# Mixture-of-experts loop of a hybrid decoder step: six whole-expert buffers, four tiles per turn in a skewed order, and no transfers for empty rows and empty blocks

## The reference

```
scores = sigmoid(t @ w_router); 64 experts in 8 groups, best 4 groups, best 8 experts per token
gates  = scores of the 8 chosen / their sum * 2.5
routed = sum over experts e: gates[:, e] * ((silu(t @ wg[e]) * (t @ wu[e])) @ wd[e])     # wg, wu 1024x256, wd 256x1024
shared = (silu(t @ w_sh_gate) * (t @ w_sh_up)) @ w_sh_down
x      = layernorm(alpha * x + g2 * (routed + shared))
```

## Time and profile before

| | |
|---|---|
| runs | 1959.46, 1959.55, 1952.16 us |
| profiled execution | 1952.46 us, span from first to last instruction 1950.6 us |
| the expert loop | from about 1137 us (first gate_up) to 1848.7 us |
| granted PE clock, mean over the span | 0.944 of full speed |

### The profile page before, as it was taken

How to read it: one execution, slowest core, us unless ns; L and a number is a source line. 1 busy time by engine, 2 the same in 40 slices (tenths; PEclk the granted TensorE clock), 3 DMA queues, 4 the chain that set the end, 5 groups by cost and what they waited for, 6 DMA issues and landing times.

```text
span 1950.6 us, 24171 instructions
## 1 busy us (share of the span) xinstructions
PE 1675.7 (86%) x8176; PEld 1041.8 (53%) x8176; DVE 639.6 (33%) x1421; ACT 408.3 (21%) x855; POOL 310.6 (16%) x571
## 2 busy tenths in 40 slices
PE   5999779988999899999969878888888888888713
PEld 2854558577857767888858633333333333333303
DVE  1213860587058842000145421111111111111186
ACT  1204431353135443000021111111111111111102
POOL 0002420255013400000001411111111111111100
PEclk8999889999999999999987989999999999999956
DMA  9113431211120083411011469999999999999681
GB/s 405 46 51 123 176 138 44 87 46 36 56 87 3 20 330 131 170 47 43 11 43 43 173 257 401 413 395 403 416 412 405 398 414 394 421 399 417 264 349 44
DMA packets 51051, 414.84 MB, mean 213 GB/s; under 512 B 5764, under 2 KB 9476, under 8 KB 23572
## 3 DMA queue, kind: packets, MB, share of 16 engines
q1 hardware_dynamic: 34276, 358.31, 46.3%
q0 software_dynamic: 14976, 54.50, 7.1%
q10 hardware_dynamic: 1728, 1.05, 0.2%
HBM read 372.91 MB, written 40.93 MB: 212 GB/s over the span
## 4 chain that ended last, share of the span: by engine, by line
PE 69%; DVE 13%; ACT 7%; issue 5%; DMA 3%; POOL 2%; ACTq 0%; SPq 0%; DVEq 0%; POOLq 0%
PE ps L1065 18%; PE ps L922 11%; PE ps L1086 10%; PE ps L883 9%; PE ps L868 7%; PE ps L954 3%; DVE work L1453 2%; DVE OA L1839 2%; ACT work L605 2%; ACT work L603 2%; DVE work L1442 1%; PE ps L839 1%; DMA W<-wq 1%; DVE work L1819 1%; PE ps L1077 1%
## 5 line engine op out<-in xcount | busy, mean ns | idle before, releaser
L1065 PE MATMUL ps<-W,work 128*64 128x512 f32 (+1 forms) x1200 | 357.0, 598 | 1.5 <-ACT work L1244 1.5
L1086 PE MATMUL ps<-work 128*64 128x512 f32 (+1 forms) x600 | 196.7, 639 | 64.1 <-ACT work L1259 64.1
L1065 PEld LDWEIGHTS ps<-W,work 128*64 128x64 f32 (+1 forms) x1200 | 129.9, 155 | 225.0 <-issue 225.0
L883 PE MATMUL ps<-Hb,W 128*128 128x260 f32 x768 | 172.9, 389 | 0.0
L883 PEld LDWEIGHTS ps<-Hb,W 128*128 128x128 f32 x768 | 148.5, 194 | 24.0 <-ACT work L1147 0.6
L1827 DVE COPY work<-ps 128x512 f32<-128x512 f32 x100 | 69.1, 691 | 269.0 <-PE ps L1086 269.0
L1086 PEld LDWEIGHTS ps<-work 128*64 128x64 f32 (+1 forms) x600 | 71.8, 163 | 157.9 <-issue 157.9
L1276 POOL TENSOR_TENSOR work<-work 128x128 f32<-128x128 f32 x168 | 82.8, 525 | 380.7 <-ACT work L605 380.3
L1250 ACT ACTIVATE work<-ps 128x256 f32<-128x256 f32 x50 | 19.2, 383 | 591.8 <-PE ps L1065 591.8
L1819 DVE TENSOR_TENSOR work<-ps,work 128x256 f32<-128x256 f32 x50 | 21.2, 424 | 358.6 <-ACT work L1250 358.6
L868 PE MATMUL ps<-W,Hb 128*128 128x512 f32 (+1 forms) x320 | 138.4, 592 | 0.0
(11 more groups left out here) (285 smaller groups left out, 2032.2 us busy)
## 6 DMA issues: line engine op xcount, KB each, us to landing
W<-wexp SPq DMA_DIRECT2D x76, 2048.0 KB, 11.8
work<-wexp SPq DMA_DIRECT2D x76, 1024.0 KB, 10.7
W<-wq SPq DMA_DIRECT2D x36, 2048.0 KB, 8.0
W<-yrows SPq DMA_DIRECT2D x6, 2048.0 KB, 16.9
work<-st_in SPq DMA_DIRECT2D x8, 1024.0 KB, 9.3
st_out<-work SPq DMA_DIRECT2D x8, 1024.0 KB, 7.1
Xb<-xT SPq DMA_DIRECT2D x2, 2080.0 KB, 17.9
work<-yrows SPq DMA_DIRECT2D x2, 2048.0 KB
```

The source lines that it names most:

```text
L883: mm = pe.matmul(ps[:, bank, 0:HALF], ring[:, q % 4, a, c, :], H[:, c, halves[b][0]:halves[b][1]], start=(c == 0), stop=(c == KC - 1))
L1065: mm = pe.matmul(ps[at, k, :], xe[:, k, c, at], GU[:, slot, c, :], start=(c == 0), stop=(c == KC - 1))
L1086: mm = pe.matmul(ps[at, 4 + hf, :], aT[:, k, f, at], WD[:, slot, f, hf * 512:(hf + 1) * 512], start=(f == 0), stop=(f == 1))
```

## The change

1. **One piece of memory.** `W`, `Hb`, `OA`, `OB` and `work` become views of one buffer `room`. Its first 6 * 6144 columns are six expert slots, each with gate, up and down weights. These lie over `Hb`, `OA` and most of `OB` too, so the sorted gate factors `gk` move to `ints`, and the shared expert's result is kept in a tensor `shrows` in memory: it is stored ahead of the loop and read back after it.
2. **One load per expert** (3.146 MB, rows of 24 KB in place of 16 KB and 8 KB). A turn of the loop has four tiles (pair, half, pair, half) in slots 0, (2, 3), 1 and (4, 5). A slot is loaded anew when the down product of the tile that used it is done. The loop has 13 turns, the last one written out apart: 52 tiles in place of 50, and places for 78 experts in place of 75.
3. **Loads that are left out.** A block without an expert has the number 64, and the load has the condition `e < NE`. From the same token numbers I count 73 loads that are made and 5 that are not. Four of those five are of the last turn, where two of the four tiles are empty.
4. **Rows that are left out.** Gather and scatter have a bound, and rows whose index lies beyond it are not moved.
5. **The order in a turn.** PE does the transposes of tile t, gate_up of t+1, turn of t+2, and then the down product of t. ACT, DVE and POOL follow this order; POOL gathers one tile further ahead.
6. The DVE steps that count the turns are written anew, with two more steps on single values. The shared expert's weights come in one load, issued one weight group earlier.

PE in the loop, before: gate_up and the turn of the next tile stand ahead of the transposes and the down product. L1065 is gate_up, L1050 the turn, L1077 the transposes of the product, L1086 the down product; a rest of the same shape is written as `x7`.

Before, the two rows of L786 stood there alone. The core of the diff:

```diff
-        W = sb("W", 4 * 4096)
+        room = sb("room", 4 * 4096 + 3 * KC * NT + 16480)
+        GU = [view(room, EW * s, 4096, "p (c f) -> p c f", c=KC) for s in range(6)]
+        WD = [view(room, EW * s + 4096, 2048, "p (f d) -> p f d", f=2) for s in range(6)]
+        SLOTS = [(0,), (2, 3), (1,), (4, 5)]
@@ sync
+            def load_expert(n, slot):
+                e = sp.value_load(eti[0:1, at], min_val=0, max_val=NE)
+                sp.dma_start(room[:, EW * slot:EW * (slot + 1)],
+                             wexp[bass.ds(e, 1), :, :].rearrange("a p n -> (a p) n"), cond=e < NE).then_inc(s_we[slot], 16)
+            load_tile(0, 0)
+            sp.wait_ge(t_hh, 4)
+            sp.wait_ge(s_ht, 2 * TT)
+            load_tile(0, 1)
+            for t in range(TT):
+                sp.wait_ge(t_yc, 2 * t + 2)
+                sp.dma_start(shrows[t * P:t * P + n, :], yb[0:n, t % 2, :]).then_inc(t_st[t % 2], 16)
+            load_tile(0, 2)
+            rows_stored(sp)
+            sp.wait_ge(s_abp, 40)
+            sp.wait_ge(s_gk8, 1)
+            load_tile(0, 3)
             with sp.Fori(1, nq) as i:
+                for k in range(4):
+                    gate(sp, "sp", s_y, i * 8 + (2 * k + 2))
+                    load_tile(i, k)
+            for t in range(TT):
+                sp.dma_start(rows_[t][0:n, :], shrows[t * P:t * P + n, :]).then_inc(t_back, 16)
@@ tensor
+            def tiles(i, last):
+                for k in range(4):
+                    ... transposes of tile 4i+k
+                    if not (last and k == 3):
+                        gate_up(i * 4 + (k + 1), (k + 1) % 4, i * 16 + (16 if k < 3 else 32))
+                    if not (last and k >= 2):
+                        turn(i * 4 + (k + 2), k % 2, i * 32 + 16 * ((k + 2) // 2 + 1))
+                    ... down product of tile 4i+k
@@ gpsimd
+                    pool.indirect_dma_start(out=xg[k], ..., bounds_check=NT - 1, oob_is_err=False)
+                    pool.indirect_dma_start(out=yrows, ..., bounds_check=YTRASH - 1, oob_is_err=False)
```

More of the change, by code:

```diff
@@ L1064, in gate_up @@
                     for at, slot in parts(k):
[L1065 removed]
+                        mm = pe.matmul(ps[at, k % 2, :], xe[:, k % 2, c, at], GU[slot][:, c, :], start=(c == 0), stop=(c == KC - 1))
                 mm.then_inc(s_hh, 1)
[L1068 to L1074 removed]
+            def tiles(i, last):
+                for k in range(4):
+                    t = i * 4 + k
+                    gate(pe, "pe", s_a, i * 4 + (k + 3))
@@ L1087, in _ @@
                                                start=(f == 0), stop=(f == 1))
                         mm.then_inc(s_y, 1)
+            turn(0, 0, 16)
+            gate_up(0, 0, 16)
+            turn(1, 1, 16)
+            with pe.Fori(0, end) as i:
+                tiles(i, False)
+            tiles(end, True)
             for m, t in enumerate(TAIL):
@@ L1252, in _, with tiles @@
             take_x(0, 0)
-            with act.Fori(0, nq) as i:
-                for k in range(2):
-                    silu(i * 2 + k, k)
-                    take_x(i * 2 + (k + 1), 1 - k)
-                    gate(act, "act", s_at, i * 2 + (k + 1))
-                    gate(act, "act", s_y, i * 4 + (2 * k + 6))
-                    act.activation(aT[:, k, :, :].rearrange("p f n -> p (f n)"), ps[:, 2, 0:2 * P], ACT.Copy).then_inc(s_ac, 1)
+            def tiles(i, last):
+                for k in range(4):
+                    gate(act, "act", s_at, i * 4 + (k + 1))
+                    gate(act, "act", s_y, i * 8 + (2 * k + 6))
+                    act.activation(aT[:, k % 2, :, :].rearrange("p f n -> p (f n)"), ps[:, 2, 0:2 * P], ACT.Copy).then_inc(s_ac, 1)
+                    if not (last and k == 3):
+                        silu(i * 4 + (k + 1), (k + 1) % 2)
+                    if not (last and k >= 2):
+                        take_x(i * 4 + (k + 2), k % 2)
+            silu(0, 0)
+            take_x(1, 1)
+            with act.Fori(0, end) as i:
+                tiles(i, False)
+            tiles(end, True)
             layer_norm_act(act, 1)
@@ L1819, in gated, with tiles @@
                 dve.tensor_tensor(av[:, k, :], ps[:, k, FE:2 * FE], sg[:, k, :], ALU.mult).then_inc(s_a, 1)
-            with dve.Fori(0, nq) as i:
-                for k in range(2):
-                    gated(i * 2 + k, k)
-                    gate(dve, "dve", s_add, i * 32 + (16 * k + 16))
-                    for hf in range(2):
-                        gate(dve, "dve", s_y, i * 4 + (2 * k + hf + 9))
-                        dve.tensor_copy(yb[:, k, hf * 512:(hf + 1) * 512], ps[:, 4 + hf, :]).then_inc(s_yc, 1)
+            def tiles(i, last):
+                for k in range(4):
+                    if not (last and k == 3):
+                        gated(i * 4 + (k + 1), (k + 1) % 2)
+                    gate(dve, "dve", s_add, i * 64 + (16 * k + 16))
+                    for hf in range(2):
+                        gate(dve, "dve", s_y, i * 8 + (2 * k + hf + 9))
+                        dve.tensor_copy(yb[:, k % 2, hf * 512:(hf + 1) * 512], ps[:, 4 + hf, :]).then_inc(s_yc, 1)
+            gated(0, 0)
+            with dve.Fori(0, end) as i:
+                tiles(i, False)
+            tiles(end, True)
+            dve.wait_ge(t_back, 16 * TT)
             def total(m):
```

172 lines of the change are left out of this document (80 added, 92 removed).

## The result

The changed kernel took 2020.12 us as the median of four runs (2014.12 to 2023.18), the kernel before 1958.87 on the same chip. The ratio is 1.0325, with a 95% interval of 1.0305 to 1.0345. It is 3.2% slower. I had forecast 1902 us and given "slower" 0.09. Two executions, one of rows4k (2489.89 us) and one of the kernel before (9573.01 us), stand far outside the others and are in none of the ratios.

The account below looks back on a forecast made before the run. PE with two short waits paced the old loop; transfers at 420 GB/s were to bound the new one. Loop -60.7, late rows +4, tables +0.4, after the loop +3.6 gave -52.7 and, with 2 us added for run spread, 1902 us; range 1870 to 1942.

Parts of the forecast that it names:

- late rows: Gathers and scatters in the loop: full tiles late by some 2 us, 4 us in all, bounds 0 and 29.
- the 15.6 us that I gave the gather: In the loop, time from a gather's issue, 3.8 us after a down product, until it is wanted, 19.4 after it.
- A late row lets the loads run ahead: In the loop, a late row gives the expert loads a lead, so late rows count only 4 us in all.
- my sum: Loop end at 1788.0 by landed loads plus PE's remaining work, -60.7 us; with the other parts -52.7.
- PE's tile: PE's time for one tile in the loop after the change: 12.0 us, 1.9 less than before.
- rival 2: PE governs the loop: transfers reach 429 GB/s or the first turn's head start is worth more; 1879 us, chance 0.12.
- Start: Tables ahead of the loop: two more DVE steps of 0.16 us, 0.4 us with what lies between.
- End: After the loop: first sum waits for shared rows, 5.1 us; empty last tile's scatter saves 1.5; net +3.6.
- What would make it wrong: Signs in the loop: PE waits for gathers, rate off 414 to 429, or gap between tiles stays at 13.9.
- The first: Rows govern: gathers and scatters in q0 hold each loop tile up by 0.6 us, 29 us; 1927 us, chance 0.13.
- The third: Rows beyond the bound still move, +40 us, 1942; with left-out loads moved too +7, 1949; chance 0.06.
- The fourth: Slower: loop transfers run at 357 GB/s, so 235.5 MB need 660 us; 2001 us, chance 0.09.

Follow-up runs that it names:

- rows4k: The changed kernel with each expert load cut into six loads of 1024 columns, so weight rows are 4 KB instead of 24 KB: 1945.37 us, ratio 0.9935.
- all_rows: The changed kernel without the bounds on gather and scatter, so every row is moved: 2027.56 us, ratio 1.0359.
- gather_none: The changed kernel with a bound of 0 on the gather, so nearly all rows are left out and products use stale rows: 2012.49 us in one run.
- row-length runs: The changed kernel with expert loads cut into shorter rows: 4 KB 1945.37 us, 16 and 8 KB 1928.05 us, 12 KB 1927.25 us.
- rows16k8k: The changed kernel with each expert load cut into gate and up weights (16 KB rows) and down weights (8 KB rows): 1928.05 us, ratio 0.9851.
- tail run: rows16k8k with each block of shared rows read just ahead of its sums' rows after the loop: 1921.26 us, ratio 0.9811.
- after: The changed kernel itself, with the whole change made to the kernel before: 2020.12 us, ratio 1.0325.

## Why the prediction was wrong

**The step that failed is "late rows", +4 us.** It stood in the sum with the right mechanism. I scaled the landing with the length of a turn, which gives 17.9 and 13.9 us for a gather and a scatter of all rows; measured with all rows (all_rows) are 20.5 for the late gathers and 13.5. But I then multiplied by 0.65 as if a left-out row took no turn, got 12.4 and 9.8, and put the step at 4 with bounds of 0 and 29. The packets above show a left-out row take a turn like any other, and a half tile's gather of almost nothing takes 19.0 us (gather_none) against 19.7, so beside rows of 24 KB that factor is near 1. My base of 11.2 us was a median over two kinds as well, and I took the full pair tiles for the late ones; it is the half tiles' gathers, with which two loads are under way. With the 15.6 us that I gave the gather, waits of 2 to 3 us followed from my own figures, where the timeline has 4.79 (19.8 less 15.0). The row-length runs take back 92 us of the loss by that cause alone.

**"A late row lets the loads run ahead" had the wrong sign.** A load waits for a down product. When PE pauses, slots come free late, and the share falls to 0.21 for 4 us. I had two costs of a pause at nothing: the loads that are not issued, and PE's clock. The second was to be read in the earlier trace rows, where a down product takes 5.35 us in place of 3.65, and in the earlier trace rows, where clocks below 1.00 stand beside stretches in which PE was less busy; in the pause above it is 2.25 us.

**What bounds the new loop.** I said transfers, at 420 GB/s. Of the changed kernel this is false. Of rows16k8k it is true, at 409: 235.5 MB then need 576 us and not 561. Its loop takes 676.6 us, against 655.1 by my sum (1788.0 + 4 less 1136.89): 15 of the 21.5 us are the rate, and 6 I can't place.

**By terms.** Between the span of 1897.9 that I summed and 2020.3 lie 122.4 us: 114.5 in the loop; 6.1 at the start (0.4 forecast, 6.5 seen); 1.8 at the end (3.6 and 5.4).
- *PE's tile*, 12.0: right, 11.8. The floor of rival 2 was 1879; without loads the kernel took 1868.
- *Start.* In the profiled executions the first gate_up starts between 1136.9 and 1141.5 for the kernel before and its two variants, and between 1137.0 and 1145.1 for the changed one and its variants. The two overlap, so part of the 6.1 us is the spread of single executions; how much isn't shown. One claim of mine was wrong: ACT's copies of the shared rows waited for their stores until 1123.96 and not 1117. This is not the row length: in rows16k8k they wait until 1123.43.
- *End.* Right in kind; the tail run takes the 5.4 us back.
- *What would make it wrong.* "If PE waits for gathers rather than for loads" was the sign named, and it is the one that came.

**The rivals.** The first had the mechanism and a quarter of its size (29 us, where the loop took 118.5 more than my sum without late rows), because it counted POOL's chain of scatters at 0.6 us a tile and not PE's wait. The third is not true: 27.00 MB in q0 and 59 loads in 39 tiles are what I counted as moved. The fourth named a slower end with a rate that falls to 357, and the mean rate is 349; but the rate is not the cause. While a load is under way, the slices reach 420 to 430 GB/s.

**The rule on turns.** The Trainium skill, "DMA: Bandwidth & Descriptors", "Queues, rings and completion order", has an engine go round its queues packet by packet. The trace agrees, with 48 packets of either queue in 3 us, and so do the landings of 19.0, 12.4 and 7.9 us for rows of 24, 12 and 4 KB. The same page says under "SWDGE vs HWDGE vs iDMA", of the transfers that GpSimd builds, that a packet is preferably at most 4096 B. If that held for SP's loads too, rows of 24 KB would cost a gather no more than rows of 4 KB. The trace disagrees for them: 182.21 MB in 8342 packets are 21.8 KB each, with the small packets that end a load counted in.

## What to carry to other kernels

When two queues share the DMA engines, the contiguous rows of the bulk loads set the latency of the small transfers beside them: here one bulk row passed for each small row, and the rows of a transfer ahead in the same queue counted too. Before loads are merged, compare that latency with the time from issue to use, and count a row that is left out as a row until a run shows otherwise. A late transfer that stops the engine which frees the buffers costs more than its wait: the clock falls, and the bulk loads stop. And fewer bytes are worth something only where the transfers are the bound, which here took both a new order and short rows.

## What the runs showed of the hardware

- Landing follows the length of a weight row: 4.3 us with no loads, then 7.9, 12.4 and 19.0 with rows of 4, 12 and 24 KB (19.7 for the late kind). An estimate from one weight row for each row of q0 comes within 0.7 us of all of them: 8 rows of a scatter and 8 of the gather behind it are 16 turns per engine; at some 425 GB/s, the rate of this run's full slices, over 16 engines, 26.6 GB/s each, and with the 2.3 us for the landing of the prediction, that is 4.8, 7.2, 12.2 and 19.5 us.
- A row beyond the bound is still a packet. In q0 after has 11266 packets for 78 transfers, some 144 each, as the kernel before has (12214 for 85). Of both queues together 5606 are under 512 B, where all_rows, which leaves none out, has 2189. From 1407 to 1410 such packets passed no faster than moved rows from 1403 to 1406, 48 in 3 us. Moving them too cost some 7 us beside 24 KB rows, and 18.3 us beside 16 and 8 KB, 40% of what their bytes are worth there.
- Full queues ran at 426 GB/s with rows of 16 and 8 KB and all rows moved, at 409 with a third of the small rows left out, and at 399 with 4 KB rows and the same rows left out.
